# Attention weights of rows 4 to 7: 32x32 block transposes on VectorE and transfers inside SBUF in place of TensorE transposes

## The chip, the cores and the metric

One core of a Trainium2 chip runs the whole kernel in one launch. The metric is the device time of the program in microseconds, from start to end. The kernel before takes 1561.25 us (median of 3 runs, 1559.95 to 1561.97).

The engines are TensorE (PE in the rows), VectorE (DVE), ScalarE (ACT), GpSimd (POOL) and SyncE (SP), which here does nothing but issue transfers. Each works through its own list of instructions in order; semaphores join the lists.

## The reference, cut to what matters

The model is one step of a two-layer trunk: a gated recurrence layer, a projection to keys and values shared by all later layers, and one forgetting-attention layer with 16 heads of 64. The part that the change touches is the attention over a prompt of 1024 tokens:

```python
def one_block(args):                      # 128 queries at a time
    qi, start = args
    s = einsum('bqhd,bkhd->bhqk', qi, k_all) * scale
    c_q = dynamic_slice_in_dim(c_t, start, q_block, axis=2)
    mask = key_pos[None, :] <= q_pos[:, None]
    logits = where(mask, s + (c_q[..., :, None] - c_t[..., None, :]), -inf)
    p = softmax(logits, axis=-1)
    return einsum('bhqk,bkhd->bqhd', p, v_all)
```

The decode part (8 sequences, each with 1024 cached keys and one new token) runs among it and isn't changed in what it computes. All data is float32.

## The kernel before

The second half of the kernel, from about 755 us on, works through 8 pairs of heads (the loop over `p`). In a pair there are 8 rows (`i`, 0 to 7): row `i` is 128 queries of both heads against `(i + 1) * 128` keys. What is done for a row:

- TensorE computes the scores into PSUM (`scores`). Rows 0 to 3 take two banks each, alternating between banks 2, 3 and 4, 5; a row from 4 on takes all of banks 2 to 5, so that its scores can only be written when the row before has left them.
- VectorE adds the bias and takes the maximum (`row_max`). ScalarE takes the exponential with its sum, the inverse of the sum by ln and exp, and multiplies (`soft`); the result goes to `weights` in SBUF.
- The product with the values needs the keys on the partitions. So TensorE transposes the weights, 128x128 at a time, back into the row's own banks (`turn_rows`, 2 (i + 1) transposes), and ScalarE (`turn_a`, first head) and VectorE (`turn_v`, second head) copy them to `pt` in SBUF.
- After each odd row TensorE multiplies two rows with the values (`weighted(p, m)`, m = 0 to 3, rows 2m and 2m + 1), and VectorE takes the result (`fin`).

Between these steps TensorE is filled with other work, in an order that is written out by hand in `pair(p)`: the projections of the next pair in products of some 2 us each (`kq` units 0 to 13 and `vg` units 0 to 13), the means for the key and query norms (`means`), the transposes of keys and values, and the decode products (`decode`, `turn_num`, `turn_top`, `spread_top`). In the last pair, which has no next pair, the filling is the output projection (`last`, `y_part`). VectorE has, besides its share of the rows, the sums of the units (`kq`, `vg`), the weights' scaling by gains (`scale_w`, four a pair), the decode scores (`score`), `norm`, and short steps (`tops`, `top_of`, `shift`, `weigh`, `smp_sum`, `smp_out`). The two pages' worth of key and value cache that a decode step needs are loaded by SP (`k_in`, one page set of 512 KB; `v_in`, four of 512 KB), each behind a wait for the buffer; GpSimd multiplies keys by queries (`times_q`) and builds sums of weights for the units (`sums_of_kq`, `sums_of_vg`).

## Time and profile before

| | |
|---|---|
| median of 3 runs | 1561.25 us |
| the profiled execution's own time | 1561.48 us |
| its span, first to last instruction | 1559.7 us |
| mean granted TensorE clock | 0.999 of full (2.4 GHz) |
| TensorE busy | 1526.2 us, 98% of the span |
| VectorE, ScalarE, GpSimd busy | 65%, 46%, 28% |
| a pair, scores of row 0 to scores of row 0 | 88.3 us |
| transposes in `turn_rows` (L2344) | 576, of which 416 in rows 4 to 7 |

An engine's busy time counts what its instructions cover; TensorE's instructions overlap, so that the pace of a run of them is read from the starts, not from the mean duration. The number behind L is a line of the kernel before. Where an engine stood idle, the brackets at the end of a line of the timeline tell how long and for whom.

### The profile page before, as it was taken

To read this page: it belongs to the slowest core of one execution; us is meant where nothing else is said; L and a number is where in the kernel's file an instruction comes from. 1 tells how busy PE (TensorE), PEld (TensorE's weight loads), DVE (VectorE), ACT (ScalarE), POOL (GpSimd) and SP (SyncE) were. 2 spreads that over 40 slices of the span, in tenths; PEclk is the share of its full clock that TensorE was granted. 3 is DMA by queue.
4 is the path that set the end of the run, shared out by engine and by line. 5 is a ranking of instruction groups with operands and counts; after the bars stand their busy time and mean duration, and the time that the engine had idled before them with its cause. 6 is when DMAs were issued, how large, how long until landed. Compare 5 with 4: busy or idle time off the path is not lost.

```text
span 1559.7 us, 23902 instructions
## 1 busy us (share of the span) xinstructions
PE 1526.2 (98%) x8769; PEld 1137.9 (73%) x8769; DVE 1013.9 (65%) x1979; ACT 713.6 (46%) x1412; POOL 430.2 (28%) x336
## 2 busy tenths in 40 slices
PE   7999999999999999999999999999999999998998
PEld 6888888888888875447777777777777777764443
DVE  5869687877868683236365877667686776766321
ACT  4445554454554542221465555555455565545100
POOL 5022212121232001012243424343343435332100
PEclk9999999999999999999999999999999999999999
DMA  9582937558292743323433445464444545365231
GB/s 274 173 252 82 278 104 209 173 154 235 79 296 97 225 169 99 88 63 100 115 89 119 126 163 176 136 203 136 159 134 134 169 161 178 149 225 216 87 135 55
DMA packets 254085, 242.32 MB, mean 155 GB/s; under 512 B 23162, under 2 KB 219962, under 8 KB 253970
## 3 DMA queue, kind: packets, MB, share of 16 engines
q1 hardware_dynamic: 242834, 204.21, 43.0%
q0 software_dynamic: 11136, 36.59, 6.7%
q8 instruction: 70, 1.15, 0.3%
q14 instruction: 45, 0.37, 0.1%
HBM read 212.63 MB, written 95.24 MB: 197 GB/s over the span
## 4 chain that ended last, share of the span: by engine, by line
PE 90%; DVE 6%; ACT 2%; issue 2%; DMA 0%; SPq 0%; POOL 0%; DVEq 0%; ACTq 0%; POOLq 0%
PE psum L2032 45%; PE psum L2056 7%; PE psum L2539 6%; PE psum L2337 4%; PE psum L2360 4%; PE psum L2344 4%; PE psum L2109 3%; PE psum L1995 2%; PE psum L2299 2%; PE psum L2393 2%; PE psum L2179 1%; PE psum L2120 1%; PE psum L2195 1%; PE psum L2207 1%; PE psum L2197 1%
## 5 line engine op out<-in xcount | busy, mean ns | idle before, releaser
L2032 PE MATMUL psum<-arena 128*128 128x252 f32 (+1 forms) x3472 | 811.3, 384 | 0.6 <-DVE arena L1358 0.6
L2032 PEld LDWEIGHTS psum<-arena 128*128 128x128 f32 x3472 | 640.7, 190 | 120.9 <-issue 30.5
L1358 DVE TENSOR_TENSOR arena<-arena,psum 128x252 f32<-128x252 f32 (+1 forms) x310 | 130.4, 421 | 204.9 <-PE psum L2032 196.2
L857 POOL TENSOR_TENSOR arena<-arena 128x1024 f32<-128x1024 f32 x64 | 160.7, 2511 | 228.2 <-DMA arena<-k_pages 210.7
L1175 ACT ACTIVATE arena<-psum,arena 128x256 f32<-128x256 f32 (+7 forms) x128 | 93.8, 739 | 120.9 <-DVE arena L1705 120.6
L934 ACT COPY arena<-psum 128x252 f32<-128x252 f32 (+1 forms) x124 | 46.0, 371 | 169.7 <-PE psum L2032 169.6
L2539 PE MATMUL psum<-arena 128*128 128x512 f32 x256 | 114.3, 597 | 0.0
L2056 PE MATMUL psum<-arena 128*128 128x512 f32 x256 | 113.0, 594 | 0.1
L720 POOL TENSOR_TENSOR arena<-arena 128x512 f32<-128x512 f32 x31 | 39.9, 1287 | 252.2 <-issue 129.3
L1184 ACT ACTIVATE arena<-arena 128x256 f32<-128x256 f32 (+7 forms) x128 | 92.4, 770 | 2.1
L2056 PEld LDWEIGHTS psum<-arena 128*128 128x128 f32 x256 | 47.5, 190 | 57.4 <-issue 56.5
L2539 PEld LDWEIGHTS psum<-arena 128*128 128x128 f32 x256 | 47.0, 190 | 56.0 <-issue 55.9
L987 ACT ACTIVATE arena<-arena 128x1024 f32<-128x1024 f32 x48 | 50.6, 1055 | 78.1 <-DVE arena L1402 78.0
L2337 PE MATMUL psum<-arena 64*128 64x512 f32 (+3 forms) x384 | 79.3, 517 | 3.1 <-DVE arena L1713 3.1
L2344 PE MATMUL psum<-arena 128*128 128x128 f32 x576 | 76.6, 276 | 5.9 <-ACT arena L1184 5.8
L2344 PEld LDWEIGHTS psum<-arena 128*128 128x128 f32 x576 | 64.7, 141 | 22.0 <-ACT arena L1184 12.6
L1713 DVE COPY arena<-psum 128x128 f32<-128x128 f32 (+3 forms) x64 | 48.4, 756 | 48.5 <-PE psum L2344 48.2
L1767 DVE TENSOR_REDUCE arena<-arena 128x16 f32<-128x1024 f32 x64 | 77.5, 1211 | 0.0
L2360 PE MATMUL psum<-arena 128*64 128x256 f32 (+1 forms) x640 | 69.5, 362 | 1.6 <-DVE arena L1819 1.6
L2360 PEld LDWEIGHTS psum<-arena 128*64 128x64 f32 x640 | 43.1, 135 | 30.2 <-issue 10.5
L1705 DVE CUSTOM_DVE_ANT_0 psum<-psum,arena 128x128 f32<-128x128 f32 (+3 forms) x128 | 63.4, 535 | 2.2
L1190 ACT COPY arena<-psum 128x128 f32<-128x128 f32 (+3 forms) x64 | 41.4, 646 | 47.1 <-PE psum L2344 45.4
(265 smaller groups left out, 2157.8 us busy)
## 6 DMA issues: line engine op xcount, KB each, us to landing
k_pages<-in_cache_k SPq DMA_DIRECT2D x64, 512.0 KB, 6.6
v_pages<-in_cache_v SPq DMA_DIRECT2D x64, 512.0 KB, 7.3
arena<-k_pages SPq DMA_DIRECT2D x64, 512.0 KB, 3.6
arena<-v_pages SPq DMA_DIRECT2D x64, 512.0 KB, 5.9
arena<-in_w_in_a SPq DMA_DIRECT2D x32, 512.0 KB, 7.0
arena<-in_x_prompt SPq DMA_DIRECT2D x16, 512.0 KB, 7.5
arena<-in_w_kv SPq DMA_DIRECT2D x16, 512.0 KB, 5.6
arena<-in_w_in_b SPq DMA_DIRECT2D x16, 512.0 KB, 7.3
```

Of the source, the lines that this page charges most:

```text
L857: pool.tensor_tensor(k_ring[:, m % 2], k_ring[:, m % 2], q_all[:, m % S:m % S + 1, :].broadcast_to([P, PAGES, P]), ALU.mult).then_inc(kq_m ...
L1175: ins = act.activation(weights[:, x, 0:n], rows[:, x, 0:n], ACT.Exp, bias=top[:, at:at + 1], scale=-1.0, accum_out=total[:, at:at + 1])
L1184: act.activation(weights[:, x, 0:n], weights[:, x, 0:n], ACT.Copy, scale=inv[:, at:at + 1]).then_inc(p_set, 1)
L1358: dve.tensor_tensor(out, more, bank[n % 2][:, 0:size(u)], ALU.add).then_inc(of.by_dve, 1)
L1705: dve.tensor_tensor_reduce(out=rows[:, x, lo:n], in0=rows[:, x, lo:n], in1=c, scale=1.0, scalar=part[:, at:at + 1] if lo else -LOW, op0=AL ...
L1767: dve.tensor_reduce(lg[:, b, :, 0:PAGES].rearrange("p x j -> p j x"), k_ring[:, m % 2].rearrange("p j (x d) -> p j x d", x=2), AX.X, ALU.a ...
L2032: ins = pe.matmul(bank[n % 2][:, 0:size(u)], w[:, k, :], x[:, k, :], start=(k == 0 and r in (0, 1, 3, 4)), stop=(k == HK - 1), skip_group_ ...
L2056: ins = pe.matmul(dst[0:rows, :], o_heads[h][:, rows_of(t)], w_o[:, h, 512 * j:512 * j + 512], start=(h == 0 or lo == AH - 1), stop=(h == ...
L2337: ins = pe.matmul(dst[:, x, lo:hi], q_t[p % 2][rows, cols(i)], k_t[p % 2][rows, lo:hi], start=True, stop=True)
L2344: ins = pe.transpose(row_banks(i)[:, x, cols(j)], weights[:, x, cols(j)], ident)
L2360: ins = pe.matmul(bank[6][rows, lo:2 * P], v_cur[:, j, rows], pt[:, x, SLOT[m] + j, lo:2 * P], start=(j == 0), stop=(j == i), skip_group_c ...
L2539: ins = pe.matmul(dst, o_y[h][:, cols(t)], w_ob[h][:, 512 * j:512 * j + 512], start=(h == 0), stop=(h == AH - 1), skip_group_check=True)
```

## The change

Rows 0 to 3 stay as they are, but for their weights, which now lie in a buffer shared with `sq[0]` (`low_weights`). For rows 4 to 7:

- ScalarE's exponential and multiplication write back into the row's PSUM banks.
- `turn_rows`, `turn_a` and `turn_v` are gone. VectorE transposes the 32x32 blocks of each head in one instruction, from PSUM into `weights` (`turn_blocks`, two a row). Each block is then transposed in itself, but still on the partitions of its queries.
- SP moves the blocks to the partitions of their keys, with 16 transfers a row from 32 partitions of `weights` to 32 partitions of `pt` (`move_row`), 64 a pair; a row of `n` = 2 (i + 1) 32 words in each, 1280 to 2048 bytes a partition. `weights` is one buffer: the transposes of a row wait until all 16 transfers of the row before have landed. `pt` of rows 4, 5 and of rows 6, 7 shares room with earlier rows, so that the transfers of rows 4 and 6 wait for `weighted(p, 1)` and `weighted(p, 2)`.
- `weighted` for rows 4 to 7 reads `pt` in runs of 32 or 128 words and waits for the transfers.

With it the orders are changed: `weighted(p, 2)` goes to the end of row 6, `weighted(p - 1, 3)` behind units 11 and 12 of the next pair, `decode(p - 1, 0)` behind the transposes of row 1; `scale_w` of keys and queries goes into row 0, of values and gates into row 3; `silu` writes the second half of the gate straight to `o_t`; `sums_of_kq` comes earlier on GpSimd.

```diff
+            def move_row(p, i):
+                sp.wait_ge(blocks_turned, 2 * high_row(p, i))
+                m, n = i // 2, block_len(i)
+                if i % 2 == 0:
+                    sp.wait_ge(pv_done, 4 * p + m)
+                at = PT_AT[m] + i % 2 * block_len(i - 1)
+                for g in range(4):
+                    for r in range(4):
+                        to = at + g * group_len(m)
+                        sp.dma_start(pt[32 * r:32 * r + 32, to:to + n], weights[32 * g:32 * g + 32, r * n:r * n + n]).then_inc(pt_moved, 16)
...
                 k_in(m + 2, m + 3)
+                move_row(p, 4)
                 if p:
                     v_in(p, 0)
                 k_in(m + 4)
+                move_row(p, 5)
...
-                k_in(m + 5, m + 6)
+                k_in(m + 5)
+                move_row(p, 6)
+                k_in(m + 6)
+                move_row(p, 7)
...
+            def turn_blocks(p, i):
+                if high_row(p, i) > 1:
+                    dve.wait_ge(pt_moved, MOVES * (high_row(p, i) - 1))
+                n = block_len(i)
+                for x in range(2):
+                    dve.wait_ge(p_set, 2 * row(p, i) - 1 + x)
+                    out = weights[:, 0:4 * n].rearrange("p (r x j l) -> p x j r l", r=4, x=2, l=32)[:, x]
+                    dve.transpose(out, row_banks(i)[:, x, 0:(i + 1) * P].rearrange("p (j r l) -> p j r l", r=4, l=32)).then_inc(blocks_turned, 1)
...
VectorE, row 3:
                 turn_v(p, 2)
+                if nxt:
+                    scale_w(dve, w_v, gain_kv, p + 1, w_v_loaded, w_v_scaled)
                 row_max(p, 3)
                 kq(3)
                 if p:
                     top_of(p - 1, 1)
+                if nxt:
+                    scale_w(dve, w_g, gain_b, p + 1, w_g_loaded, w_g_scaled)
                 kq(4)
                 fin(p, 0)
                 score(m)
                 turn_v(p, 3)
...
VectorE, row 7:
                 row_max(p, 7)
                 vg(4)
+                if nxt:
+                    top_of(p, 0)
                 vg(5)
                 score(m + 4)
                 if nxt:
                     norm(p + 1, 0)
                 vg(6)
                 last(3)
-                turn_v(p, 7)
-                top_of(p, 0)
                 if nxt:
                     norm(p + 1, 1)
                     shift(p, 0)
+                turn_blocks(p, 7)
...
ScalarE, row 7: rs_ln(p + 1, 1, 2) and rs_out(p + 1, 1) now stand ahead of soft(p, 7)
...
TensorE:
                 scores(p, 0)
-                if p:
-                    weighted(p - 1, 3)
                 vg(p, 9)
                 turn_k(p, 0)
-                if p:
-                    decode(p - 1, 0)
                 turn_rows(p, 0)
                 turn_k(p, 1)
                 vg(p, 10)
                 turn_smp(p)
                 scores(p, 1)
                 vg(p, 11, 12)
                 if p:
+                    weighted(p - 1, 3)
+                turn_rows(p, 1)
+                if p:
+                    decode(p - 1, 0)
+                vg(p, 13)
...
                 scores(p, 7)
                 means_n(1, 1)
                 vg_n(4)
                 means_n(1, 2)
+                if nxt:
+                    turn_top(p, 0)
                 vg_n(5, 6)
                 last((4, 0, 8))
-                turn_rows(p, 7)
-                if nxt:
-                    turn_top(p, 0)
-                vg_n(7)
                 if nxt:
                     spread_top(p, 0)
-                vg_n(8)
+                vg_n(7, 8)
```

## Rows read from the trace of the kernel before

**Rows 1.** The page: busy time of TensorE, and the chain that ended last by engine.

```profile
PE 1526.2 (98%) x8769; PEld 1137.9 (73%) x8769; DVE 1013.9 (65%) x1979; ACT 713.6 (46%) x1412; POOL 430.2 (28%) x336
...
PE 90%; DVE 6%; ACT 2%; issue 2%; DMA 0%; SPq 0%; POOL 0%; DVEq 0%; ACTq 0%; POOLq 0%
```

**Rows 2.** TensorE's waits: us in total, times, longest us.

```profile
PE psum L2344 <- ACT arena L1184: 5.8, 7, 1.8
PE psum L2337 <- DVE arena L1713: 3.1, 7, 1.3
PE psum L2360 <- DVE arena L1819: 1.6, 1, 1.6
```

**Rows 3.** Timeline of TensorE, one pair: start, us, line, shape, count.

```profile
1198.23 0.49 PE L2337 MATMUL psum<-arena 64*128 64x128 f32 x4
...
1232.59 1.35 PE L2337 MATMUL psum<-arena 64*128 64x512 f32 x8 [0.15 <-DVE arena L1713]
...
1242.82 1.56 PE L2337 MATMUL psum<-arena 64*128 64x512 f32 x8
...
1251.83 1.53 PE L2344 MATMUL psum<-arena 128*128 128x128 f32 x12
...
1256.96 1.77 PE L2337 MATMUL psum<-arena 64*128 64x512 f32 x8
...
1272.24 1.99 PE L2337 MATMUL psum<-arena 64*128 64x512 f32 x8
...
1280.52 1.91 PE L2344 MATMUL psum<-arena 128*128 128x128 f32 x16
1282.27 0.27 PE L2370 MATMUL psum<-arena 128*8 128x128 f32 x1
...
1286.54 0.49 PE L2337 MATMUL psum<-arena 64*128 64x128 f32 x4
```

**Rows 4.** Timeline of VectorE in rows 4 and 7 of the same pair.

```profile
1232.88 1.22 DVE L467 TENSOR_TENSOR arena<-arena 128x1024 f32<-128x1024 f32 x1
...
1239.70 1.21 DVE L1767 TENSOR_REDUCE arena<-arena 128x16 f32<-128x1024 f32 x1
1240.92 0.82 DVE L1713 COPY arena<-psum 128x640 f32<-128x640 f32 x1
...
1279.09 0.42 DVE L1358 TENSOR_TENSOR arena<-arena,psum 128x252 f32<-128x252 f32 x1 [1.86 <-PE psum L2032]
1279.43 1.21 DVE L1767 TENSOR_REDUCE arena<-arena 128x16 f32<-128x1024 f32 x1
1280.56 1.28 DVE L1671 SCALAR_TENSOR_TENSOR arena<-arena 128x1032 f32<-128x1032 f32 x1
...
1282.47 1.23 DVE L1713 COPY arena<-psum 128x1024 f32<-128x1024 f32 x1 [0.30 <-PE psum L2344]
```

**Rows 5.** Timeline of ScalarE: row 0 of that pair, a mean in row 7.

```profile
1201.11 0.37 ACT L1175 ACTIVATE arena<-psum,arena 128x128 f32<-128x128 f32 x1 [3.46 <-DVE arena L1705]
...
1202.43 0.69 ACT L1184 ACTIVATE arena<-arena 128x128 f32<-128x128 f32 x2
...
1275.04 0.55 ACT L1113 ACTIVATE arena<-psum,arena 128x344 f32<-128x344 f32 x1 [1.20 <-PE psum L2299]
```

**Rows 6.** Timeline of SP: two issues of four transfers of 512 KB.

```profile
1029.32 1.75 SPq L587 DMA_DIRECT2D arena<-v_pages  x4
...
1206.58 2.56 SPq L587 DMA_DIRECT2D arena<-v_pages  x4
```

**Rows 7.** Transfers, KB each, us from issue to landing: 985 to 1005, and 0 to 31 us.

```profile
arena<-v_pages SPq DMA_DIRECT2D x4, 512.0 KB, 6.4
...
arena<-in_w_kv SPq DMA_DIRECT2D x1, 512.0 KB, 7.4
...
arena<-in_g_norm_a SPq DMA_DIRECT2D x1, 0.5 KB, 2.2
```

**Rows 8.** Timeline of VectorE at the start: the kernel's one transpose on it.

```profile
1.81 0.31 DVE L1299 STREAM_TRANSPOSE arena<-arena 128x128 f32<-128x128 f32 x1
```

More of the change, by code:

```diff
@@ L485, in row_banks, with low_row, high_row, low_pt @@
             return psum[:, 512 * at:512 * at + 2 * width].rearrange("p (x n) -> p x n", x=2)
+        def low_row(p, i):
+            return LOW_ROWS * p + i + 1
+        def high_row(p, i):
+            return LOW_ROWS * p + i - LOW_ROWS + 1
+        def low_pt(i, x):
+            if i < 2:
+                at, step = (0, 128)[i] * 2 + x * P * (i + 1), P
+            else:
+                at, step = PT_AT[1] + x * 8 * P + (i - 2) * P, 2 * P
+            return bass.AP(pt.tensor, pt.offset + at, [pt.ap[0], [step, i + 1], [1, P]])
+        def block_len(i):
+            return 2 * (i + 1) * 32
+        def group_len(m):
+            return block_len(2 * m) + block_len(2 * m + 1)
+        def moving(m, x, j):
+            first, both = 2 * m, j <= 2 * m
+            if m == 0:
+                at, row_step, inner = x * P, 2 * P + x * P, [[1, P]]
+                at, row_step = (at, row_step) if both else (2 * P + x * 2 * P + P, 0)
+            elif m == 1:
+                at, row_step, inner = PT_AT[1] + x * 8 * P + j * 2 * P + (0 if both else P), P, [[1, P]]
+            else:
+                row_step, inner = block_len(first) + 32 * x, [[group_len(m), 4], [1, 32]]
+                at = PT_AT[m] + x * 32 * (first + 1) + 32 * j + (0 if both else row_step)
+            return bass.AP(pt.tensor, pt.offset + at, [pt.ap[0], *([[row_step, 2]] if both else []), *inner])
         PIECES = [1 + (i >= TT // 2) for i in range(TT)]
@@ L672, in last @@
                 resb_in(1)
-                k_in(m + 5, m + 6)
+                move_row(p, 5)
+                k_in(m + 5)
+                move_row(p, 6)
+                k_in(m + 6)
+                move_row(p, 7)
                 resb_in(2)
@@ L1169, in soft @@
                 n, rows = (i + 1) * P, row_banks(i)
+                dst = low_weights if i < LOW_ROWS else rows
                 for x in range(2):
@@ L1286, in _ @@
             for j in range(2):
-                strip_out(2 + j, bank[4 + j], weights[:, 0, 512 * j:512 * j + 512])
+                strip_out(2 + j, bank[4 + j], weights[:, 512 * j:512 * j + 512])
         @block.vector
@@ L1868, in _ @@
                     score(m - 2)
+                    fin(p - 1, 3)
                 turn_v(p, 1)
+                if p:
+                    smp_sum(p - 1, 0)
                 vg_add(p, 13)
@@ L1896, in _ @@
                 score(m + 1)
-                turn_v(p, 4)
+                turn_blocks(p, 4)
                 kq(8)
-                if nxt:
-                    scale_w(dve, w_g, gain_b, p + 1, w_g_loaded, w_g_scaled)
                 row_max(p, 5)
@@ L1923, in _ @@
                 last(2)
-                turn_v(p, 6)
+                turn_blocks(p, 6)
                 vg(3)
-                if p + 2 < PAIRS:
-                    scale_w(dve, w_k, gain_kv, p + 2, w_k_loaded, w_k_scaled)
+                fin(p, 2)
                 row_max(p, 7)
                 vg(4)
+                if nxt:
+                    top_of(p, 0)
                 vg(5)
@@ L1940, in _ @@
                     shift(p, 0)
+                turn_blocks(p, 7)
+                if not nxt:
+                    top_of(p, 0)
                 vg(8)
@@ L1943, in _ @@
                     new_score(p + 1)
-                if p + 2 < PAIRS:
-                    scale_w(dve, w_q, gain_b, p + 2, w_q_loaded, w_q_scaled)
             p, m = PAIRS - 1, S * PAIRS
-            fin(p, 3)
             shift(p, 0)
@@ L1952, in _ @@
             y_add(5)
+            fin(p, 3)
             score(m - 2)
@@ L2348, in weighted @@
                 i = 2 * m + 1
-                pe.wait_ge(pt_a, row(p, i))
-                pe.wait_ge(pt_v, row(p, i))
+                if i < LOW_ROWS:
+                    pe.wait_ge(pt_a, low_row(p, i))
+                    pe.wait_ge(pt_v, low_row(p, i))
+                else:
+                    pe.wait_ge(pt_moved, MOVES * high_row(p, i))
                 if m == 0:
@@ L2498, in pair @@
                 means_n(1, 0)
+                weighted(p, 2)
                 scores(p, 7)
```

112 lines of the change are left out of this document (48 added, 64 removed).

## Prediction

> **What bounds the kernel now.** I read the page first: TensorE is busy for 98% of the span, and 90% of the chain that ended last runs through it [rows 1]. So a microsecond taken from TensorE is worth a microsecond as long as nothing else ends later. The list of TensorE's waits came next: for the weights of a row, for a row's banks and for a decode step together some 10 us, most of them in the last pair [rows 2]. Then one pair in the timeline. Write s4, s5, s6, s7, s0 for the start of the scores of rows 4, 5, 6, 7 and of row 0 of the next pair. The reader is to see the distances: s4 to s5 10.2 us, s5 to s6 14.1, s6 to s7 15.3, s7 to s0 14.3, the pair 88.3 [rows 3]. TensorE fills each of them without a gap, and that filling is what a shorter or longer chain of softmax work is hidden behind. VectorE's and ScalarE's timelines say how long that chain is [rows 4, 5], SP's and the transfers' rows what a move costs [rows 6, 7].
>
> **What is removed.** The transposes of rows 4 to 7 are 10 + 12 + 14 + 16 = 52 a pair. Sixteen of them take 1282.27 - 1280.52 = 1.75 us, 0.109 each [rows 3]. So TensorE loses 1.1, 1.3 (1.4 from the start of the twelve at 1251.83 to what follows), 1.5 and 1.75 us in rows 4, 5, 6, 7: 5.7 a pair, 45.5 in eight. With nothing given back the kernel would take 1561.5 - 45.5 = 1516, and some 10 less if the waits went too. VectorE's copy and ScalarE's copy of each row go as well; VectorE's was 0.82 us in row 4 and 1.23 in row 7 [rows 4].
>
> **What is added on VectorE.** Two transposes a row from PSUM. The one transpose in the trace took 0.31 us for 128 words a partition [rows 8], and the copies from PSUM show about 1.07 ns a word above a fixed part of 0.14 [rows 4], which for 128 words is 0.28. So I price a block transpose like a copy of its size: 0.82 in row 4, 1.23 in row 7, 4.1 a pair above what the copy cost. The lower bound is that (nothing in the trace is cheaper from PSUM), the upper is twice it, since the shape with runs of 32 words out of PSUM isn't shown.
>
> **What is added on SP.** A move row is 16 issues. Four issues of `v_in` took 1.75 us, 0.44 each, or 2.56 under load, 0.64 each [rows 6]. I take 0.44, as there is mostly no load queued, hence 7.0 us a row; the last lands 2.2 us after its issue (the smallest transfer [rows 7]; upper bound the 6.4 of a big one behind others). So a row has moved 9.2 us after its transposes. Bounds: 16 x 0.44 + 2.2 = 9.2 and 16 x 0.64 + 6.4 = 16.6. The data of a row, 0.66 to 1.05 MB, is less than what four `v_in` carry in that time, so the issue sets the pace.
>
> **Row 4.** VectorE's order there hangs on TensorE through `fin(p, 1)`, then comes `gate_in`, then `score`, begun at 1239.70, and the copy at 1240.92, which is 8.3 us after s4 = 1232.59 [rows 3, 4]. In its place two transposes end at 8.3 + 0.7 + 0.8 + 0.1 = 9.95. TensorE would be ready at 10.2 - 1.1 = 9.1, so it waits 0.8: of 1.1 us 0.2 stays.
>
> **Row 5.** The decode product ends at 1251.83, s5 + 9.0; `smp_sum` behind it ends at 9.7, the row 4 moves have landed at 9.2, two transposes end at 11.7. TensorE is ready at 14.1 - 1.4 = 12.8. All of 1.4 stays; cover 1.1 us.
>
> **Row 6.** TensorE is ready at 13.75. The row 5 moves start at s5 + 11.7, behind `v_in` and a `k_in` (2.5 MB issued from s5 + 9 on), and land at s6 + 8 to 10. The transposes end at 11.3 (VectorE has `smp_out`, unit 1, `score`, `tops` ahead). But ScalarE now takes more means ahead of `soft(p, 6)`, and TensorE's fourth mean waits for its read of the third, about 0.45 us. 1.1 of 1.5 stays.
>
> **Row 7.** Here I expect the whole gain to be lost. `turn_top` now stands right behind the last mean and shares its bank; ScalarE reads a mean just when it ends, 0.55 us [rows 5], so TensorE waits 0.8. VectorE's sum of unit 5, at 1279.09 = s7 + 6.85 before [rows 4], comes at 7.7. Behind it stand in order the rest of the sum 0.34, `score` 1.13, `norm` 1.2, sum 0.34, `norm` 1.2, `shift` 0.4 (starts in the timeline are 1.13 and 1.2 apart [rows 4]), then 1.14 + 1.23 for the transposes: s7 + 14.7, and row 0's scores wait for it. Before it was 14.3 [rows 3]. Row 7 gets 0.4 longer. The row 6 moves, begun at s7 (behind `weighted(p, 2)`), have landed at 9.2 and are covered by 3 us.
>
> **Row 0.** `weighted` (3.4 us) and `decode` (2.1) were what hid row 0's softmax; both are moved behind it. The scores now start as VectorE ends row 7's transposes, the maximum starts 0.75 later, the exponential 0.85 after that, and ScalarE needs 1202.43 + 0.35 - 1201.11 = 1.67 from there to the first head's weights [rows 5]: s0 + 3.3 and 3.6. TensorE is there at 2.7 (scores, one unit, four key transposes). It waits 0.85, and then 0.35 for ScalarE's read of the key transposes, which now comes behind `soft`: 1.2 us longer. `weighted(p - 1, 3)` comes at s0 + 12.4 against moves landed at 9.2: covered.
>
> **Row 3.** Two `scale_w` of 1.22 us [rows 4] come here from rows 4 and 5, where they cost nothing. The second stands between `top_of` and `turn_v(p, 3)`, whose copy releases the banks for row 4; TensorE waited 0.15 for that copy already [rows 3], so all of 1.1 goes on the path. The first needs the value weights, loaded behind `v_in` and a `k_in`; four-fold `v_in` 6.4 and the weights 7.4 from issue [rows 7] put their landing at the moment VectorE asks, 0 to 1 us late. Sum 1.4, bounds 0.3 (the cover elsewhere taken) and 2.3.
>
> **The sum.** Pairs 1 to 6: +1.2 + 1.4 - 0.2 - 1.4 - 1.1 + 0.4 = +0.3 each, +2. Pair 0 has no `weighted` or `decode` in row 0 to lose, and its `scale_w` leaves the front of row 0 (-1.2); with 1.1 in row 3 and less cover in row 5 (+0.3) it comes to -2. The last pair has no `scale_w`, and its filling of `y_part` is long: -1.4 and -1.5 in rows 5 and 6, -1.75 in row 7, the waits of 1.6 for `smp_out` and up to 1.3 for the bank [rows 2], 1.5 for `smp_sum`, which now stands ahead of the transposes; +1.2 in row 0 and +0.7 in row 4: -6.5. In all -6.5, from the profiled execution's 1561.5 (its own time is 0.2 above the median) to 1555; against the median 1554.8.
>
> **A rule that speaks against it.** The moves go from 32 partitions to 32. In the trace of before no transfer inside SBUF is shown, and the loads all reach 128 partitions, four of 512 KB landing in 6.4 us [rows 7]. The Trainium skill (SBUF — State Buffer, the DMA port swizzle) says that transfer bandwidth depends on how many of 16 ports the partitions reach, and a run of 32 partitions reaches 8. By its 435 GB/s for all, an estimate is 218 GB/s, 4.8 us for row 7's 1.05 MB, still below the 7 us of issue; were the landing 2.4 us later for it, row 5 would lose 0.75 us a pair and the time be 1561. No run here shows it yet.
>
> **Rivals.**
> 1. *The gain is kept.* If VectorE's lateness in rows 0, 3 and 7 costs half of what I give (my orders add up every operation ahead, and a wait at one place gives cover at the next), 3 of the 6 us a pair given back stay, 21 us in seven pairs: 1534; with nothing given back 1516. For it: TensorE at 98% and VectorE at 65% [rows 1]. Against: the rows where VectorE ends 0.3 us ahead of TensorE today.
> 2. *The moves are late* (slower). At 0.64 an issue [rows 6] a row has moved after 12.5 us; row 5's transposes then start at 12.5 and end at 14.4, 1.6 past TensorE; times 8 is 13 us, less small cover: 1568. It decides from about 0.5 us an issue, where it has eaten my gain. If moves also queue behind `v_in`, `weighted(p, 2)` waits too: 1580.
> 3. *The transposes are dear.* At 1.5 times a copy rows 4 and 7 grow by 0.8 and 1.2 us a pair, 16 in all: 1571; at twice 1587.
>
> **How the numbers follow.** 0.2% is 3.1 us, about what a measurement tells from no change. Chances: my case 0.42 (its own range 1547 to 1563), rival 1 0.22, rival 2 0.24, rival 3 0.08, else 0.04. Faster: 0.29 of my case, rival 1, 0.01: 0.52. Same: 0.09 of my case, 0.05 of rival 2, 0.01: 0.15. Slower: the rest, 0.33. For 8 in 10 I leave out the lower half of rival 1 and the ends of 2 and 3: 1532 to 1575.
>
> **What would show it.** L2344's count falls from 576 to 160. In a middle pair: s7 to s0 near 14.7 with TensorE's row 0 scores waiting for VectorE's transposes; row 4's scores waiting some 1.5 us for the copy of row 3; waits of TensorE for ScalarE in row 0; none in rows 5 and 6 beyond 0.5. A block transpose of 1024 words takes 1.2 us; 16 issues on SP take 7. The prediction is wrong if VectorE waits for transfers ahead of its transposes (rival 2), if a transpose takes 1.5 us or more (rival 3), or if rows 0 and 3 show no wait (rival 1).

## The result, and the profile after

| | before | after |
|---|---|---|
| median | 1561.07 us, remeasured beside it | 1621.72 us of 4 runs (1619.34 to 1626.99) |
| span of the profiled execution | 1559.7 us | 1625.3 us |
| mean granted TensorE clock | 0.999 | 0.982 |

The change makes the kernel slower: ratio 1.0395, 95% interval 1.0383 to 1.0408, 60.6 us. The forecast of 1555 and its range up to 1575 are both missed. The profiled execution of the kernel after is the slowest of its four (1626.99 us), so its spans stand some 5 us above the median.

The page of the kernel after, with the rows that answer to [rows 1]:

```profile
PE 1516.5 (93%) x8353; PEld 1107.2 (68%) x8353; DVE 1032.6 (64%) x2019; ACT 683.5 (42%) x1380; POOL 420.1 (26%) x336
...
PE 68%; SPq 11%; DMA 8%; DVE 7%; issue 4%; ACT 2%; POOL 0%; DVEq 0%; POOLq 0%
```

TensorE has 416 instructions fewer and is busy for only 9.7 us less; the span is 65.6 longer. The chain that ended last now runs for 11% through SP's issuing and for 8% through transfers. Both stand at 0% in [rows 1]. The waits of the second half (760 to 1625 us; engine and line, releaser, us in total, times, longest), the answer to [rows 2]:

```profile
POOL arena L916 <- DMA arena<-k_pages: 449.6, 61, 17.4
...
DVE arena L1772 <- DMA arena<-arena: 47.7, 20, 5.5
...
PE psum L2397 <- DVE arena L1772: 29.9, 20, 2.7
...
PE psum L2404 <- ACT arena L1242: 29.4, 16, 3.6
...
DVE arena L471 <- DMA arena<-in_w_kv: 20.6, 6, 4.1
...
PE psum L2423 <- DMA arena<-arena: 13.5, 10, 2.4
```

L1772 are the block transposes, L2397 the scores, L2404 `turn_rows`, L471 `scale_w`, L2423 `weighted`, L916 `times_q`. VectorE's block transposes wait for the moves of the row before, 20 times; then the scores wait for VectorE. TensorE also waits ahead of `turn_rows` (for ScalarE's weights) and ahead of `weighted` (for the moves). One middle pair in TensorE's timeline (p = 5, the pair that is read throughout), against [rows 3]:

```profile
1238.19 0.49 PE L2397 MATMUL psum<-arena 64*128 64x128 f32 x4 [1.89 <-DVE arena L1772]
...
1243.39 0.77 PE L2404 MATMUL psum<-arena 128*128 128x128 f32 x2 [1.14 <-ACT arena L1242]
...
1276.98 1.73 PE L2404 MATMUL psum<-arena 128*128 128x128 f32 x8 [2.46 <-ACT arena L1242]
...
1281.41 1.35 PE L2397 MATMUL psum<-arena 64*128 64x512 f32 x8
...
1291.96 1.56 PE L2397 MATMUL psum<-arena 64*128 64x512 f32 x8 [1.34 <-DVE arena L1772]
...
1306.17 1.77 PE L2397 MATMUL psum<-arena 64*128 64x512 f32 x8 [1.26 <-DVE arena L1772]
...
1319.54 2.65 PE L2423 MATMUL psum<-arena 128*64 128x256 f32 x24 [1.95 <-DMA arena<-arena]
1322.12 1.99 PE L2397 MATMUL psum<-arena 64*128 64x512 f32 x8
...
1337.41 0.49 PE L2397 MATMUL psum<-arena 64*128 64x128 f32 x4 [1.87 <-DVE arena L1772]
```

From start of scores to start of scores, row by row, us. "Forecast" is the distance of [rows 3] with the prediction's term; the last two columns are runs told below:

| stretch | before | forecast | after | four moves | four moves, scale back |
|---|---|---|---|---|---|
| rows 0 and 1 | 17.75 | 18.95 | 22.45 | 19.34 | 19.34 |
| row 2 | 8.14 | 8.14 | 8.15 | 8.15 | 8.14 |
| row 3 | 8.47 | 9.87 | 12.62 | 13.38 | 8.47 |
| row 4 | 10.23 | 10.0 | 10.55 | 10.53 | 9.88 |
| row 5 | 14.14 | 12.75 | 14.21 | 12.88 | 12.87 |
| row 6 | 15.28 | 14.2 | 15.95 | 13.93 | 13.93 |
| row 7 | 14.3 | 14.7 | 15.29 | 14.82 | 14.83 |
| the pair | 88.3 | 88.6 | 99.2 | 93.0 | 87.5 |

Pairs 1 to 6 together are 593.7 us after and 532.9 before: 60.8 of the 65.6 us. The rest is 0.4 in pair 0, 2.5 from row 0 to row 7 of the last pair, and 1.9 behind that. The pair read before is one of the shortest: pairs 1 to 6 took 88.3 to 89.6 us before (row 3 8.5 to 9.6) and 97.6 to 99.7 after.

SP's issues for the moves of the pair before that one, p = 4 (start, us for all issues of the group), which answer to [rows 6]:

```profile
1192.89 10.85 SPq L666 DMA_DIRECT2D arena<-arena  x16
...
1206.98 10.04 SPq L666 DMA_DIRECT2D arena<-arena  x16
...
1223.03 11.19 SPq L666 DMA_DIRECT2D arena<-arena  x16
1234.26 0.58 SPq L618 DMA_DIRECT2D arena<-k_pages  x1
1238.07 10.01 SPq L666 DMA_DIRECT2D arena<-arena  x16
```

Sixteen moves take 10.0 to 11.2 us to issue, 0.63 to 0.70 each, where I took 7.0. They land 2.1 us after issue in the median, as I took, but not all of them: in pairs 1 to 6 the last move of row 5 lands 2.8 to 3.9 us after its issue, beside loads of 512 KB. The block transposes by shape, against the copies of [rows 4] (count, then busy us and mean ns):

```profile
L1772 DVE STREAM_TRANSPOSE arena<-psum 128x1024 f32<-128x1024 f32 x16 | 19.0, 1228 | 6.8 <-DMA arena<-arena 6.8
...
L1772 DVE STREAM_TRANSPOSE arena<-psum 128x640 f32<-128x640 f32 x16 | 12.5, 820 | 0.0
```

These are 1.23 and 0.82 us, the price of a copy to the hundredth. Rival 3 is out. In the experiments below a ratio is to the kernel before measured beside it, with its 95% interval in brackets.

### The profile page after: what moved, and what is told of

The parts are those of the page before. It is cut to its first block, busy times and chain, and to the rows that moved or that the text cites. A ratio compares the mean times of both kernels' runs of the same rounds, so it can differ in the third digit from the quotient of the medians.

```text
span 1625.3 us, 23526 instructions
## 1 busy us (share of the span) xinstructions
PE 1516.5 (93%) x8353; PEld 1107.2 (68%) x8353; DVE 1032.6 (64%) x2019; ACT 683.5 (42%) x1380; POOL 420.1 (26%) x336
## 4 chain that ended last, share of the span: by engine, by line
PE 68%; SPq 11%; DMA 8%; DVE 7%; issue 4%; ACT 2%; POOL 0%; DVEq 0%; POOLq 0%
PE psum L2090 32%; SPq L666 10%; PE psum L2114 7%; PE psum L2596 5%; DMA arena<-in_w_kv 4%; PE psum L2423 4%; PE psum L2167 3%; DMA arena<-arena 3%; PE psum L2397 2%; DVE arena L1772 2%; PE psum L2053 2%; PE psum L2455 2%; DVE arena L1826 1%; PE psum L2237 1%; PE psum L2253 1%
## 5 line engine op out<-in xcount | busy, mean ns | idle before, releaser
L2090 PE MATMUL psum<-arena 128*128 128x252 f32 (+1 forms) x3472 | 824.2, 389 | 0.6 <-DVE arena L1408 0.6
L916 POOL TENSOR_TENSOR arena<-arena 128x1024 f32<-128x1024 f32 x64 | 151.4, 2366 | 454.4 <-DMA arena<-k_pages 449.6
L2596 PE MATMUL psum<-arena 128*128 128x512 f32 x256 | 118.7, 616 | 5.7 <-DVE arena L1818 3.6
L2114 PE MATMUL psum<-arena 128*128 128x512 f32 x256 | 113.0, 594 | 0.1
L2397 PE MATMUL psum<-arena 64*128 64x512 f32 (+3 forms) x384 | 81.2, 527 | 31.6 <-DVE arena L1772 29.9
L1772 DVE STREAM_TRANSPOSE arena<-psum 128x640 f32<-128x640 f32 (+3 forms) x64 | 63.3, 1027 | 47.7 <-DMA arena<-arena 47.7
L1233 ACT ACTIVATE arena<-psum,arena 128x128 f32<-128x128 f32 (+3 forms) x64 | 33.2, 523 | 133.0 <-DVE arena L1755 133.0
L2423 PE MATMUL psum<-arena 128*64 128x256 f32 (+1 forms) x640 | 70.3, 364 | 13.5 <-DMA arena<-arena 13.5
L1233 ACT ACTIVATE psum<-psum,arena 128x640 f32<-128x640 f32 (+3 forms) x64 | 59.1, 924 | 49.6 <-DVE arena L1755 49.6
L2397 PEld LDWEIGHTS psum<-arena 64*128 64x128 f32 x384 | 32.7, 188 | 68.8 <-issue 43.6
L2423 PEld LDWEIGHTS psum<-arena 128*64 128x64 f32 x640 | 42.6, 134 | 46.8 <-DMA arena<-arena 18.8
L1744 DVE CUSTOM_DVE_ANT_0 psum<-psum,arena 128x512 f32<-128x512 f32 x64 | 43.1, 716 | 29.8 <-PE psum L2397 29.8
```

The lines of the kernel that those rows point to most:

```text
L916: pool.tensor_tensor(k_ring[:, m % 2], k_ring[:, m % 2], q_all[:, m % S:m % S + 1, :].broadcast_to([P, PAGES, P]), ALU.mult).then_inc(kq_m ...
L1233: ins = act.activation(dst[:, x, 0:n], rows[:, x, 0:n], ACT.Exp, bias=top[:, at:at + 1], scale=-1.0, accum_out=total[:, at:at + 1])
L1772: dve.transpose(out, row_banks(i)[:, x, 0:(i + 1) * P].rearrange("p (j r l) -> p j r l", r=4, l=32)).then_inc(blocks_turned, 1)
L2090: ins = pe.matmul(bank[n % 2][:, 0:size(u)], w[:, k, :], x[:, k, :], start=(k == 0 and r in (0, 1, 3, 4)), stop=(k == HK - 1), skip_group_ ...
L2114: ins = pe.matmul(dst[0:rows, :], o_heads[h][:, rows_of(t)], w_o[:, h, 512 * j:512 * j + 512], start=(h == 0 or lo == AH - 1), stop=(h == ...
L2397: ins = pe.matmul(dst[:, x, lo:hi], q_t[p % 2][rows, cols(i)], k_t[p % 2][rows, lo:hi], start=True, stop=True)
```

## The experiments

**The price of an issue, measured alone.** The kernel's work is left out; one queue at a time issues a group of transfers, waits for all, and goes on.

```diff
+            for i in range(16):   # L234: 32 partitions x 1280 B; L237 the same with 2048 B
+                sp.dma_start(b[32 * (i % 4):32 * (i % 4) + 32, ...], a[32 * (i // 4):32 * (i // 4) + 32, ...])
+            # L240 4 loads from DRAM to 128 partitions, 512 KB; L243 4 moves of 128 partitions inside SBUF, 256 KB
+            # L246 16 loads from DRAM to 32 partitions; L249 16 moves onto the same partitions
+            # L257, L265: the 16 of L237 from ScalarE's and GpSimd's queue
```

> The kernel does nothing of the reference: it issues groups of transfers with nothing else running, each group after the one before has landed. On SP: 16 moves inside SBUF from 32 partitions to 32 others with 1280 bytes a partition, 16 with 2048 bytes, 4 loads from DRAM of 512 KB to 128 partitions, 4 copies inside SBUF over 128 partitions with 2048 bytes, 16 loads from DRAM to 32 partitions with 1280 bytes, 16 moves that stay on their partitions; then the 2048-byte moves on ScalarE's and on GpSimd's queue. Theory A (an issue of a transfer inside SBUF costs SP more than one of a load, whatever else runs): 0.6 to 0.7 us a move here too, 10 to 11 us a group of 16, against 0.44 a load. Rival (the price comes from other transfers queued in the whole kernel): 0.44 a move, 7 us a group, as I had put it. Both expect a last landing some 2 us behind the last issue.

Measured, the timelines of SP, ScalarE's queue and GpSimd (`a`, `b` are in SBUF, `rows` in DRAM):

```profile
15.74 10.11 SPq L234 DMA_DIRECT2D b<-a  x16
27.19 10.01 SPq L237 DMA_DIRECT2D b<-a  x16
38.66 1.76 SPq L240 DMA_DIRECT2D b<-rows  x4
46.94 2.48 SPq L243 DMA_DIRECT2D b<-a  x4
51.37 7.29 SPq L246 DMA_DIRECT2D b<-rows  x16
60.13 10.06 SPq L249 DMA_DIRECT2D b<-a  x16
```

```profile
71.58 10.16 ACTq L257 DMA_DIRECT2D b<-a  x16
```

```profile
83.52 7.95 POOL L265 DMA_DIRECT2D b<-a  x16 [83.08 <-ACTq L213]
```

An issue of a transfer inside SBUF costs 0.63 us on SP, for each size and number of partitions tried (0.62 at 128 partitions). From DRAM it costs 0.44 to 128 partitions and 0.46 to 32. ScalarE's queue pays 0.64, GpSimd 0.50. The 0.64 of [rows 6] is the same number by accident: those were loads from DRAM, and what made them dearer than 0.44 is not shown. (Loads of the same kind also come dearer elsewhere: four `v_in` took 4.29 us to issue in the run with the loads first.)

**The scale back where it was.** `scale_w` of values and gates goes from row 3 to rows 4 and 5, as before the change.

```diff
 VectorE, row 3:
-                if nxt:
-                    scale_w(dve, w_v, gain_kv, p + 1, w_v_loaded, w_v_scaled)
...
-                if nxt:
-                    scale_w(dve, w_g, gain_b, p + 1, w_g_loaded, w_g_scaled)
 row 4:
                 kq(5)
+                if nxt:
+                    scale_w(dve, w_v, gain_kv, p + 1, w_v_loaded, w_v_scaled)
...
                 turn_blocks(p, 4)
                 kq(8)
+                if nxt:
+                    scale_w(dve, w_g, gain_b, p + 1, w_g_loaded, w_g_scaled)
```

> The changed kernel with one part undone: VectorE's scaling of the value and gate weights goes back from row 3 to rows 4 and 5, where it was before. Theory B (a large share of the loss is row 3, where VectorE waits 3 to 4 us for the value weights and TensorE for it, at half its clock): row 3, 12.6 to 13.0 us from scores to scores now, falls to about 8.5 to 9, rows 4 and 5 grow by at most 1 together, 20 to 27 us in seven pairs, 1595 to 1602 us. Theory A alone (the moves on SP set the pace, slack of row 3 is eaten behind them): less than 8 us, 1614 or more.

Measured: 1587.01 us, ratio 1.0185 [1.0159, 1.0212], clock 0.995. Row 3 falls to 8.46 us, rows 0 and 1 stay at 21.6, the pair is 92.3. So the place of `scale_w` costs about 35 us of the 60. The time is 8 us below the range foretold, as rows 4 and 5 did not grow (9.87 and 14.16 us). The 26 us that are left above the kernel before come with the moves.

**The weights loaded first.** In SP's order the loads of the value and gate weights go ahead of `v_in(p - 1, 1)` and `k_in(m)`.

```diff
                 if p:
                     k_in(m - 1)
-                    v_in(p - 1, 1)
-                    k_in(m)
                 sp.wait_ge(b_units.done, vg_b(p, 14))
                 load_wb(sp, w_v, w_kv_d, p + 1, 1, w_v_loaded)
                 load_wb(sp, w_g, w_qg_d, p + 1, 1, w_g_loaded)
+                if p:
+                    v_in(p - 1, 1)
+                    k_in(m)
```

> The changed kernel with the order of SP changed in pairs 1 to 6: the loads of the next pair's value and gate weights stand ahead of the four value-cache loads and one key-cache load, not behind them. Theory B says that the wait in row 3 is for bytes queued ahead of the weights: they then land some 6 us after issue in place of 10.3, VectorE doesn't wait for them, 2.5 to 3.5 us a pair in six pairs, 15 to 21 us, 1601 to 1607 us. If instead the place of the scaling on VectorE (1.2 us each in the way) is what costs, this gains less than 5 us while undoing it gains 20. Rival: the later value-cache loads delay the decode product; then TensorE waits for them in row 5 and the time stays.

Measured: 1621.39 us, 1.0389 [1.0356, 1.0422], clock 0.986: nothing gained. VectorE no longer waits for the weights (it did, 20.6 us in all), and row 3 of the pair read is 10.28 us in place of 12.62. But the keys' load is now the late one; in row 3 of that pair VectorE's decode score waits for GpSimd's product:

```profile
1274.41 1.22 DVE L1827 TENSOR_REDUCE arena<-arena 128x16 f32<-128x1024 f32 x1 [1.72 <-POOL arena L917]
```

TensorE then stands 1.97 us ahead of row 4's scores, waiting for VectorE's copy. Row 4 is longer in all of pairs 1 to 6 (11.1 to 13.8 against 10.3 to 11.5). In both orders tried, the load that goes last is late for something that stands in VectorE's order; how much of row 3's remaining 1.8 us is the scaling's own 1.2 and how much the late keys is not separated.

**Four moves in place of sixteen.** Each move takes 128 partitions straight across, the same bytes. Rows 4 to 7 then multiply with keys out of place, so their output differs.

```diff
-MOVES = 16 * 16
+MOVES = 16 * 4
...
                 for g in range(4):
-                    for r in range(4):
-                        sp.dma_start(pt[32 * r:32 * r + 32, to:to + n], weights[32 * g:32 * g + 32, r * n:r * n + n])...
+                    sp.dma_start(pt[:, to:to + n], weights[:, g * n:g * n + n])...
```

> The changed kernel with 4 transfers a row in place of 16, each over 128 partitions and with the same bytes in all; the blocks stay on their partitions, so the attention output of rows 4 to 7 is another. Theory A: SP then needs 2.6 us a row in place of 10.5, VectorE's 48 us of waits for moves and TensorE's 13 for them go, loads behind them start 8 us earlier; rows 5 and 6 fall by 1.3 and 1.7 us to 12.9 and 14.2, row 3 by 0 to 1: 25 to 35 us, 1587 to 1597. If bytes and not issues set the pace of a move, nothing changes in the waits for moves and the time stays within 5 us of 1622. What my own forecast had without late moves, 1555, would need rows 0 and 3 to be as I had put them, and they were not: this run does not get there.

Measured: 1583.05 us, 1.0145 [1.0128, 1.0162], clock 0.990. All but one of VectorE's waits for moves are gone (1.7 us in all, 47.7 before), rows 5, 6 and 7 take 12.88, 13.93 and 14.82. Row 3 does not fall, as the run's forecast had it, but grows, in pairs 1 to 6 to 13.1 to 15.5 us (12.1 to 13.7 with sixteen moves): VectorE's waits for the value weights are still there, 23.0 us in all. Row 0's stretch falls from 9.73 to 6.62: there `new_score` took 2.40 us beside a late `times_q` on GpSimd, and 0.47 here. The two rows of the kernel after, VectorE and GpSimd, and then VectorE's with four moves:

```profile
1238.28 2.40 DVE L1730 TENSOR_TENSOR arena<-arena 64x8 f32<-64x8 f32 x2
```

```profile
1238.14 2.35 POOL L916 TENSOR_TENSOR arena<-arena 128x1024 f32<-128x1024 f32 x1 [10.46 <-DMA arena<-k_pages]
```

```profile
1212.87 0.47 DVE L1729 TENSOR_TENSOR arena<-arena 64x8 f32<-64x8 f32 x2
```

**Both edits.**

> Both edits at once: four moves a row over all 128 partitions in place of sixteen (rows 4 to 7 then meet keys out of place, so their output differs), and the scale of the next pair's value and gate weights back where it was. If the loss has these two causes and they add up, the distances between the starts of the scores over a middle pair are the smaller of the two runs' for each row: 6.6, 12.7, 8.1, 8.5, 9.9, 12.9, 13.9 and 14.8, which is 87.4 us a pair against 92.3 and 93.0 with one edit alone and 88.3 before: 1546 to 1553 us, 8 to 15 below the kernel before, and a granted clock back at 0.995 or more. If the clock's fall or the transposes themselves cost something that neither edit takes away, it stays at 1565 or more.

Measured: 1543.78 us, 0.9897 [0.9882, 0.9912], clock 0.999, middle pairs of 87.5 to 87.7 us. In the middle pairs the two causes account for the whole loss: every stretch has the length foretold. The time itself is 2 us below the range foretold. Without TensorE's transposes and with the longer chain on VectorE, the kernel would be 16 us below the kernel before, if the moves of a row cost four issues. This version doesn't compute the reference. Four moves in place of sixteen change the partitions that a transfer touches besides the number of issues; the run above shows that an issue costs the same either way.

**Half the moves on GpSimd** (with the scale back, the output whole). GpSimd issues groups 2 and 3 of each row, with a semaphore of its own; SP issues groups 0 and 1.

```diff
+            def pool_moves(p, i):
+                pool.wait_ge(blocks_turned, 2 * high_row(p, i))
+                ...
+                for g in range(2, 4):
+                    for r in range(4):
+                        pool.dma_start(...).then_inc(pt_moved_p, 16)
...
                 if p + 1 < PAIRS:
                     sums_of_vg(p + 1)
+                pool_moves(p, 4)
-                times_q(m + 3, m + 4)
+                times_q(m + 3)
+                pool_moves(p, 5)
+                times_q(m + 4)
...
+                pool_moves(p, 6)
                 times_q(m + 5)
+                pool_moves(p, 7)
```

> Half of each row's moves go out from GpSimd's queue (0.50 us each there, by the price measured alone) while SyncE issues the other half (0.63 each); scale back as in the run of that name; nothing is left out. Issues as the cause: a row's moves then take 5 us in place of 10 on either queue, rows 6, 7 and 0 each give back 1 to 2 us of the 92.3 us pair: about 88 us a pair, 1553 to 1562 us. The rival, that GpSimd's products for the queries of the next row are now late behind its own moves and its waits: row 6 or row 7 grows by the 5 us of issues in part, and the time stays at 1575 or above.

Measured: 1616.33 us, 1.0352 [1.0336, 1.0368], clock 0.978. Worse than the scale back alone, and the rival as to the outcome, but at another row than it named: row 5 takes 19 us. GpSimd's timeline there, and VectorE's:

```profile
1284.26 1.68 POOL L783 TENSOR_TENSOR arena<-arena 128x512 f32<-128x512 f32 x1
1285.89 4.01 POOL L929 DMA_DIRECT2D arena<-arena  x8
```

```profile
1276.74 1.57 DVE L1790 STREAM_TRANSPOSE arena<-psum 128x640 f32<-128x640 f32 x2
...
1295.51 1.85 DVE L1790 STREAM_TRANSPOSE arena<-psum 128x768 f32<-128x768 f32 x2 [7.08 <-issue]
```

The transposes of row 4 ended at 1278.31. SP's half left at 1278.34, GpSimd's at 1285.89, behind four sums (`sums_of_vg`) of 5.9 us. These eight moves landed after 4.8 us in the median and 6.2 at most, beside four `v_in` that SP issued from 1287.51 on; over the whole trace GpSimd's moves land after 2.2 us in the median and SP's after 2.4, so it is not GpSimd's queue that makes them land late. Row 5's transposes stood for 7.08 us: the profile names no releaser for that wait, but the last of the eight landed at 1295.43, 0.08 us before they began.

**A unit as cover in row 0** (with the scale back).

```diff
                 turn_k(p, 0)
+                vg(p, 10)
                 turn_rows(p, 0)
                 turn_k(p, 1)
-                vg(p, 10)
```

> Scale back, and one unit of the value and gate projection moved ahead of the turning of row 0, as cover while VectorE finishes the new score. If TensorE stands only because row 0 has too little work before its turn, about 1 to 2 us a pair come back from the 13.1 us between the scores of rows 1 and 2 or from the 8.5 before: 1573 to 1580 us. If the late product on GpSimd and the moves that precede its load on SyncE set that stretch, the wait only shifts, and the time stays at 1584 to 1590.

Measured: 1587.87 us, 1.0182 [1.0165, 1.0199], no difference from 1587.01. Row 0's stretch is shorter (6.8 to 7.6 us in pairs 1 to 7, 7.7 to 10.1 before) and row 1's longer (13.6 to 16.9 against 12.7 to 13.9); in the pair read TensorE waits 1.60 us for moves ahead of `weighted(p - 1, 3)`. The wait shifted, as the second branch of the forecast has it; the cover was not what was short.

**The three edits together.**

> The three edits that leave the output whole: half the moves on GpSimd, the scale back, the unit ahead of the turning of row 0. If the causes add up: 1548 to 1558 us, below the kernel before by 3 to 13 us. If GpSimd's queue becomes late as in the rival to the half-and-half run, 1570 or more.

Measured: 1615.28 us, 1.0353 [1.0339, 1.0367]: as the half on GpSimd without the unit moved. Row 5 is again 18.9 to 20.7 us.

**Row 4 whole on SP.** As half on GpSimd, but GpSimd begins at row 5; and a second kernel in which it begins at row 6.

```diff
-                for g in range(2):
+                for g in range(4 if i < HALVED else 2):   # HALVED is 5, or 6
...
-                pool_moves(p, 4)
```

> Scale back; GpSimd issues half of the moves of rows 5, 6 and 7, SyncE all sixteen of row 4; nothing is left out. In the half-and-half run the moves of row 4 left GpSimd 7.5 us late, behind its four products for the prompt (6 us), and VectorE's turn of row 5 waited 7.1 us for them. If that queue was all that was wrong, the distances between scores are 6.6, 12.7, 8.1, 8.5, 9.9, 13 to 14, 14 and 14.8, which is 87.7 to 88.7 us a pair: 1547 to 1557 us. If descriptors from GpSimd or its moves' landings (4.8 us in the median of one stretch, against 2) are themselves too slow, rows 6 and 7 stay at 15 us or more and the time at 1575 or above.

> As the other run of this call, but GpSimd issues half of the moves of rows 6 and 7 alone. Row 5 to 6 then keeps the 14.2 us of the run with the scale back, rows 6 and 7 give back 1.3 and the stretch of row 0 1.8: 88.9 to 90 us a pair, 1557 to 1567 us. Again 1575 or more if moves from GpSimd cost more than the queue that they relieve.

Measured: 1565.07 us, 1.0026 [1.0014, 1.0038] from row 5 on, and 1578.99, 1.0122 [1.0105, 1.014] from row 6 on. Middle pairs are 88.5 to 88.9 and 89.5 to 90.7 us. With GpSimd from row 5 on, rows 6, 7 and 0 are in most pairs as short as with four moves (13.93, 14.83, 6.62), and row 5 takes 13.8 to 14.3. The place of row 4's moves in GpSimd's queue is thus what was wrong with half on GpSimd. The second kernel misses its forecast of 1557 to 1567 by 12 us; its profile is of its fastest execution (1571.27), so that its pairs are shorter than in most. The middle pairs of the first are as foretold (within 0.3 us), its time is not: it loses 3.7 us to four moves in pair 0 (83.4 against 79.7) and 6.1 in the last pair from row 5 to row 7 (35.1 against 29.0). In the last pair SP issued the two loads of the residual's rows at 1428.87, behind row 4's sixteen moves; VectorE waited 3.65 us for them, and TensorE 5.20 for VectorE and then ran a group of 16 matmuls in 8.8 us in place of 7.1.

**Row 4 first on GpSimd**, and then **the residual's rows first on SP** as well:

```diff
+                pool_moves(p, 4)
                 if p + 1 < PAIRS:
                     sums_of_vg(p + 1)
-                pool_moves(p, 4)
...
 SP, last pair:
                 k_in(m + 3)
+                resb_in(0)
+                resb_in(1)
                 move_row(p, 4)
```

> The half-and-half run with scale back (1616 us), with one thing moved: GpSimd issues its half of row 4's moves ahead of its four products for the next pair, not behind them. Nothing is left out. If the 7.1 us for which VectorE waited there was that queue alone, the distance from row 5 to row 6 falls from 19 to 12.9 to 13.5, row 6 to 7 to 13.9, and the clock stays at 0.995 or more: 87.5 to 88.3 us a middle pair against 88.6 with all of row 4 on SyncE, 1552 to 1560 us. If the products, 4 us later, are what the next pair's projection waits for, row 6 or 7 grows by 2 us or more and it stays at 1565 or above.

> As the other run of this call, and in the last pair the two loads of the residual's rows leave SyncE ahead of row 4's moves instead of behind them. VectorE waited 3.65 us for them there and TensorE 5.2, and its next 16 matmuls then ran at half the clock, 8.8 in place of 7.1 us. If that is the loads' place alone: 3 to 6 us below the other run, 1548 to 1555. If they only collide with the values' loads elsewhere: within 1 us of it.

Measured: 1571.2 us, 1.0064 [1.0051, 1.0078], and 1568.49, 1.0041 [1.0027, 1.0055]; what the second edit brings is not told apart from nothing (the intervals overlap). Both stand above their forecasts, by 11 and 13 us. The traces say why the second brings nothing: in the last pair TensorE waits ahead of the same 16 matmuls 3.62 us without it and 3.61 with it. In neither does VectorE wait for the residual's rows ahead of them; a small product of two SBUF operands stood beside GpSimd's product each time, first without the edit, then with it:

```profile
1436.56 2.21 DVE L1894 TENSOR_TENSOR arena<-arena 64x4 f32<-64x4 f32 x1
```

```profile
1440.31 2.20 DVE L1825 TENSOR_TENSOR arena<-arena 128x8 f32<-128x8 f32 x1
```

Behind these equal waits the 16 matmuls took 7.13 us at a granted clock of 1.00 in the first profile, and 9.80 in the second, where the clock fell to 0.50. In the middle pairs row 5 falls from 19 to 14.8 us, not to 12.9 (in one pair of six it does). GpSimd's sums, 4 us later, now begin within 0.3 us of a product of VectorE's `silu`:

```profile
1246.62 3.32 DVE L1811 TENSOR_TENSOR arena<-arena 128x512 f32<-128x512 f32 x1
```

```profile
1246.89 1.28 POOL L780 TENSOR_TENSOR arena<-arena 128x512 f32<-128x512 f32 x1
1248.11 1.27 POOL L781 TENSOR_TENSOR arena<-arena 128x512 f32<-128x512 f32 x1
```

The product of 128x512 took 3.32 us beside two of GpSimd's, and 0.68 in the half-and-half run, where GpSimd's product at that place took 1.72 in place of 1.27. So one of the two is held. Both times VectorE's product is recorded as the earlier, by 0.27 us here and 0.08 there; what decides which is held is not shown. TensorE waits 1.64 us for VectorE behind it. The forecast named that move as a risk, with the next pair's projection as the victim; it was VectorE.

**VectorE beside GpSimd, measured alone.** The kernel's work is left out. VectorE runs groups of operations; GpSimd multiplies 128x1024 inside SBUF.

> Not the kernel's work: VectorE runs groups of three float32 products of 128x512 inside SBUF, six products of 64x4 inside SBUF, three products of SBUF by PSUM, three turns of 32x32 blocks from PSUM, three copies from PSUM; first alone, then the same groups while GpSimd runs three products of 128x1024 (2.36 us each). If a VectorE operation with two operands in SBUF is held until GpSimd's running product ends, the products inside SBUF come out at about 2.4 to 3.3 us for the first one or for each, against 0.68 (128x512) and 0.15 (64x4) alone, while turns and copies from PSUM keep their 0.8 and 0.6 us. If the stalls in the kernels had another cause (a transfer, a PSUM bank, the order of waits), all groups take the same beside GpSimd as alone, within 0.1 us.

Measured, VectorE's timeline and then GpSimd's (`a`, `b`, `c`, `d` in SBUF, `ps` in PSUM):

```profile
5.22 1.90 DVE L246 TENSOR_TENSOR b<-a 128x512 f32<-128x512 f32 x3
7.03 0.51 DVE L251 TENSOR_TENSOR b<-a 64x4 f32<-64x4 f32 x6
7.47 1.87 DVE L256 TENSOR_TENSOR b<-a,ps 128x512 f32<-128x512 f32 x3
9.26 1.90 DVE L261 STREAM_TRANSPOSE b<-ps 128x512 f32<-128x512 f32 x3
11.09 1.84 DVE L271 COPY b<-ps 128x512 f32<-128x512 f32 x3
12.87 6.75 DVE L246 TENSOR_TENSOR b<-a 128x512 f32<-128x512 f32 x3
19.54 4.36 DVE L251 TENSOR_TENSOR b<-a 64x4 f32<-64x4 f32 x6
```

```profile
7.53 41.72 POOL L233 TENSOR_TENSOR d<-c 128x1024 f32<-128x1024 f32 x18 [3.28 <-DVEq L279]
```

GpSimd began at 7.53, earlier than meant, so that only the first two groups ran alone. Beside it the same groups take 6.75 us in place of 1.90 and 4.36 in place of 0.51. Of the other three groups there is no run alone here. Beside GpSimd a product with PSUM takes 0.67 us, a block transpose 0.67 to 0.72 and a copy from PSUM 0.65 to 0.69; the product inside SBUF alone takes 0.69, and copies of that size in the kernel before 0.67 to 0.69, so they are not held. GpSimd is held too: its products take up to 2.35 us beside those three groups and up to 2.79 beside VectorE's products inside SBUF. The expectation had it that a product waits once, 2.4 to 3.3 us; each of the three of 128x512 was held (1.70, 2.38, 2.82), but of the six small ones two (2.29, 1.85).

## Why the prediction was wrong

**Issues.** The step that failed is "I take 0.44, as there is mostly no load queued, hence 7.0 us a row". A move costs 0.63 with nothing else running, hence 10 us; the row that I had read was of loads from DRAM. Rival 2 had this number, by the accident told above, and the point at about 0.5 from which it decides; I gave it 0.24. For row 5 it says 1.6 us past TensorE; measured are 14.21 against 12.88 with short issues, 1.3. Its second branch, `weighted(p, 2)` waiting as well, is there too (1.95 us in the pair read), and with the scaling back where it was the kernel takes 1587 where that branch says 1580. What neither I nor rival 2 had is that the issues also stand in SP's queue: the keys for row 0's decode step leave behind row 6's moves at 1234.26, GpSimd's product comes at 1238.14, and VectorE's small product is held by it until TensorE has waited 1.14 us (0.37 with four moves) and fallen to half its clock. Rows 0 and 1 cost 3.1 us of the pair that way, rows 6 and 7 2.5 (15.95 and 15.29 against 13.93 and 14.82). In row 6 a part is not issue but landing: the last move of row 5 left SP at 1315.58 and landed at 1319.50, 3.9 us later in place of 2.0, and that is the 1.95 us for which TensorE stood. The rule on ports that I weighed is not what made it late: moves of the same shape land after 2.1 us in the median, and this one went out beside loads. (I had also written that the loads before all reach 128 partitions; `in_x_sample` reaches 8. Nothing rests on it.)

**Row 3.** The step that failed is the landing of the value weights, "0 to 1 us late". Its price was taken from [rows 7] and its start was not followed through SP's queue. `v_in` waits for the decode step that the change moves behind row 1. It left SP at s0 + 8.35 before and leaves at s0 + 20.5 (1258.69), right behind `decode`; the weights behind it leave at 1260.97, share the transfers with it and land 10.3 us later. VectorE stands for 2.92 us, in front of all of row 3's softmax:

```profile
1271.34 1.74 DVE L471 TENSOR_TENSOR arena<-arena 128x1024 f32<-128x1024 f32 x1 [2.92 <-DMA arena<-in_w_kv]
```

TensorE waits 2.46 us for it at `turn_rows(p, 3)`. Against a bound of 2.3, row 3 grew by 4.2 us: the wait, and 1.5 us because the eight transposes and the unit behind it take 4.43 us to row 4's scores where they took 2.90. The 1.1 us that I had put on row 4's scores for the second `scale_w` is not seen there (they wait 0, 0.15 before); it shows only with the loads first, where they wait 1.97.

**The clock.** I had no term for it. Windows over the pair's start (length; busy us of TensorE, its loads, VectorE, ScalarE, GpSimd; granted clock; share and GB/s of transfers):

```profile
1234.00:1238.00 4.00, 2.30 (x11) 1.62 (x9) 3.56 (x6) 1.03 (x3) 0.00 (x0) 1.00 0.56 160
1238.00:1242.00 4.00, 3.81 (x16) 2.95 (x16) 3.90 (x11) 0.38 (x3) 2.35 (x1) 0.72 0.32 79
1242.00:1246.00 4.00, 2.86 (x11) 2.00 (x10) 2.86 (x4) 3.04 (x11) 0.00 (x0) 0.50 0.40 101
```

The granted clock falls to 0.50, the level of 1.2 GHz, behind the 4 us in which TensorE was busy for 2.3; nearly all of its wait of 1.89 us for the transposes lies in them. Eight products of a unit then take 2.78 and 2.71 us where they take 2.05 at 2.4 GHz, 0.7 each time; row 3 has such a stretch too (2.97). With both causes gone TensorE waits 1.40 us at the same place, the windows there stay at 1.00, and the mean clock is 0.999 again. So the fall comes with the longer waits and adds to them; that it doesn't come behind each wait of a given length is seen in the 7.13 and 9.80 us above.

**What held.** The removed transposes; the price of a block transpose; rows 0 and 1 (18.95 against 19.34), row 4 (10.0, 9.88), row 5 (12.75, 12.87), row 6 (14.2, 13.93) and row 7 (14.7, 14.83), all in the run with both causes gone; its pair is 87.5 against 88.6 - 1.4 = 87.2 by my terms without row 3's. In rows 4 and 7 the waits are those foretold as well (0.67 for 0.8 ahead of row 5's scores, 0.64 for 0.8 at `turn_top`). In rows 0 and 1 the sum came near in part by luck: they grew by 1.6 us for my 1.2, but with waits of 0.5; the other 1.1 is TensorE's pace in the new order, as in the four transposes of row 1, which take 0.64 us to the next start where they took 0.44. The loss came from what I had put at nothing: SP's queue as a resource that other work passes through. The 60.8 us of pairs 1 to 6 are 10.1 a pair. The scale back alone takes 35 us off the whole, short issues alone 39, and both together 78, against a sum of 73. In pair 0 and the last pair, where I forecast -2 and -6.5, the four moves with the scale back gave 79.7 against 84.0 and 71.1 against 77.4 to row 7; what took that gain was mostly the issues (short issues alone: 80.1 and 71.4). My -2 for pair 0 was itself less than half of the 4.3 that were there.

**What stays open.** How much the clock costs by itself was not measured; no run keeps the waits and the clock. No version with the right output beats the kernel before: the best, GpSimd from row 5 on, is 0.3% slower. Whether ScalarE's queue could take a few issues of row 4 was not tried.

## What to carry to other kernels

Count the issues of a queue like work on an engine, with the price for their source and destination, and follow every load that stands behind them to the instruction that needs it. Where a step is moved, follow the buffers that it frees: the load that waits for them moves too. Before putting a VectorE product of two SBUF operands on a path, look at what GpSimd does at that moment. And before taking a price from a row, look whether the row is of the same kind of transfer.

## What the runs showed of the hardware

- With nothing else running, a transfer's issue on SP took 0.63 us inside SBUF and 0.44 to 0.46 from DRAM; ScalarE's queue took 0.64 and GpSimd 0.50 for the moves. 1280 or 2048 bytes a partition (10.11 and 10.01 us for 16) and 32 or 128 partitions (0.63 and 0.62) made no difference.
- VectorE's products with both operands in SBUF were held by GpSimd's product (1.90 to 6.75 us, 0.51 to 4.36), those with an operand in PSUM were not (0.67 us each beside it). By the Trainium skill (SBUF — State Buffer, the section "SBUF: two separate sides") the pair of ports is an exclusive lock, also against a VectorE operation with two SBUF inputs when GpSimd reads SBUF; the measurement agrees in that both sides were held (GpSimd's products up to 2.79 us beside VectorE's, up to 2.35 otherwise).
- A block transpose from PSUM took what a copy took, 0.82 us for 640 words a partition and 1.23 for 1024.
